# Gate slabs of experts 4 to 15 requested by ScalarE on its own DMA queue

## The chip, the cores and the metric

The kernel runs on one core of a Trainium2 chip. The metric is device time in microseconds (us) of one execution. Work is spread over TensorE (PE), VectorE (DVE), ScalarE (ACT), GpSimd (POOL) and SyncE (SP), and over 16 DMA engines which carry data from HBM into the on-chip memory. SP does no arithmetic here: it waits for semaphores and issues DMA transfers. In the order listings below "ACT" is ScalarE, and a wait `slab_free0` is the semaphore that says that buffer 0 may be overwritten.

## The reference

Two blocks of two layers each, on 256 tokens of width 1024, all in float32. The change touches only the mixture of experts of the first block:

```
def expert_choice_moe(h, w_router, w_gate, w_up, w_down):
    ...
    gates, idx = lax.top_k(aff.transpose(0, 2, 1), cap)      # 16 experts, 32 tokens each
    xs = h[b_ix, idx]
    a = jnp.einsum('becd,edf->becf', xs, w_gate)
    u = jnp.einsum('becd,edf->becf', xs, w_up)
    y = jnp.einsum('becf,efd->becd', jax.nn.silu(a) * u, w_down)
    y = y * gates[..., None].astype(y.dtype)
    return jnp.zeros_like(h).at[b_ix, idx].add(y)
```

Each layer has 16 experts, each with a gate, an up and a down matrix of 1024 x 1024 float32 (4 MB). Before the experts a layer has token mixing, attention over a memory and a router; after the two layers a second block follows, of another kind, with dense matrices.

## The kernel before

**Slabs and slots.** Every matrix of an expert is read as two slabs of 2 MB (2048 KB in the profile), in which each of the 128 partitions gets 16 KB in one piece. The slabs go into a ring of six slots. Gate slabs use slots 0 and 1 (`GATE_SLOTS` is 2), up slabs slots 2 and 3, down slabs slots 4 and 5 (`LAST_SLOT`). So there is one expert's worth of slots, and a slab of the next expert can be asked for as soon as the matmuls that read the slot's old content are done: TensorE then raises `m.free[slot]`, and `ring_wait` waits for it. A transfer raises `m.landed[slot]` by 16 when its last piece is in, and TensorE waits for that (`slab_landed`).

**SP's order.** All slabs are asked for by SP, in one fixed order: `sync_first`, and in it `expert_slabs(e)` for the experts 3 to 14: up, up, down, down of expert e, then gate, gate of expert e+1. Each issue waits for its own slot, so a slot that isn't free holds up all that stand behind it. In layer 0 the loop is written out, and after the experts 3 and 8 two slabs of the next layer's memory weights are asked for (`memory_weights`, 4 KB pieces); in layer 1 it is a loop in registers (`Fori`). Expert 15's up and down slabs follow outside the loop, its second down slab in two halves (`last_down_half`), and then the first slabs of what comes after the experts.

**TensorE's order.** `tensor_experts` runs for expert e: transposes of the gating weights (`turn_places`), then the gate and up products as one nest, k from 0 to 7 outside and the four groups g inside (g 0 and 1 gate, g 2 and 3 up; line 1639). k 0 to 3 need slots 0 and 2, k 4 to 7 need slots 1 and 3. Slots 0 and 2 are free after k = 3, slots 1 and 3 after k = 7. Then it gathers the next expert's tokens, transposes the products, waits for the activation, and runs the down products (line 1673: 16 matmul records for slot 4, 16 for slot 5) and `combine` (line 1683), which adds the expert's rows into the sums of all tokens. In layer 0 the experts 5 to 8 and 11 to 14 are preceded by a piece of other work (`memory_job`, keys and values of the next layer), 7 us on TensorE.

The last expert has an order of its own, `last_gate_up` (line 1568): gate products of k 0 to 3 (slot 0), gate products of k 4 and 5 (slot 1), then, with slot 2, the gate products of k 6 and 7 and the up products of k 0 to 3, then, with slot 3, the up products of k 4 to 7. Its down products for the second slab are done by halves, and `combine` of the first half starts the work that follows the experts.

**ScalarE's order.** `expert` in `scalar_first`: it copies the products out of PSUM (`gu_rows`), applies Silu to the transposed gate products (waits for `gu_T`), and copies the first half of the down product (waits for `dn_full`). TensorE waits for all three. In layer 0 the experts are written out, in layer 1 experts 0 to 14 are a `Fori` loop.

## Time and profile before

| | us |
|---|---|
| median of 3 runs | 2149.88 |
| lowest, highest run | 2148.53, 2151.23 |
| profiled execution, device time | 2150.17 |
| its span (first to last instruction) | 2148.3 |
| TensorE busy in the span | 1886.7 (88%) |
| ScalarE busy | 705.4 (33%) |
| chain that ended last: TensorE | 61% |
| chain that ended last: DMA | 29% |
| of it `w_up` slabs, `w_down` slabs | 17%, 11% |

The chain that ended last is followed back from the end, at each step to what released the waiting instruction. It names what the time went by, so a resource that is busy but not on it costs nothing. The device time is 1.9 us above the span, and the profiled execution lies 0.3 us above the median.

### The profile page before, as it was taken

To read this page: it belongs to the slowest core of one execution; us is meant where nothing else is said; L and a number is where in the kernel's file an instruction comes from. 1 tells how busy PE (TensorE), PEld (TensorE's weight loads), DVE (VectorE), ACT (ScalarE), POOL (GpSimd) and SP (SyncE) were. 2 spreads that over 40 slices of the span, in tenths; PEclk is the share of its full clock that TensorE was granted. 3 is DMA by queue.
4 is the path that set the end of the run, shared out by engine and by line. 5 is a ranking of instruction groups with operands and counts; after the bars stand their busy time and mean duration, and the time that the engine had idled before them with its cause. 6 is when DMAs were issued, how large, how long until landed. Compare 5 with 4: busy or idle time off the path is not lost.

```text
span 2148.3 us, 37589 instructions
## 1 busy us (share of the span) xinstructions
PE 1886.7 (88%) x16744; PEld 1279.0 (60%) x16744; DVE 915.5 (43%) x1340; ACT 705.4 (33%) x1023; POOL 45.7 (2%) x68
## 2 busy tenths in 40 slices
PE   9999958857888999866676689999999999999998
PEld 7897314322325795312222248677999886779997
DVE  7644200101014654101110138458676574486774
ACT  6644100000003653111111135325544454255443
POOL 1000000000000100000000000000000000000000
PEclk9999989989999999988888899999999999999999
DMA  9266999999999358999999995032853360228540
GB/s 340 99 252 254 421 424 427 426 425 428 427 428 390 122 224 345 428 429 428 427 428 429 429 398 185 4 127 94 263 196 138 123 228 4 93 106 276 187 157 20
DMA packets 140159, 592.53 MB, mean 276 GB/s; under 512 B 5840, under 2 KB 59296, under 8 KB 114672
## 3 DMA queue, kind: packets, MB, share of 16 engines
q1 hardware_dynamic: 138912, 586.68, 68.9%
q0 software_dynamic: 1104, 3.70, 0.5%
q8 instruction: 120, 1.97, 0.4%
q14 instruction: 23, 0.19, 0.0%
HBM read 589.30 MB, written 1.05 MB: 275 GB/s over the span
## 4 chain that ended last, share of the span: by engine, by line
PE 61%; DMA 29%; DVE 4%; ACT 2%; SPq 2%; issue 1%; DVEq 0%; POOL 0%; POOLq 0%; ACTq 0%
PE ps L653 37%; DMA ring<-in_w_up 17%; DMA ring<-in_w_down 11%; PE ps L1639 7%; PE ps L3171 3%; PE ps L1673 2%; PE ps L1683 1%; PE ps L3220 1%; SPq L883 1%; PE ps L670 1%; DVE ring_lo L629 1%; DMA area<-in_mem 1%; ACT slab_hi L624 1%; PE ps L3318 1%; PE ps L1212 1%
## 5 line engine op out<-in xcount | busy, mean ns | idle before, releaser
L1639 PE MATMUL ps<-ring,area 128*32 128x512 f32 x1728 | 271.9, 677 | 158.3 <-DMA ring<-in_w_up 157.5
L629 DVE TENSOR_TENSOR ring_lo<-ring,slab_hi 128x2048 fp32r<-128x2048 f32 (+2 forms) x137 | 302.8, 2212 | 182.1 <-ACT slab_hi L624 182.0
L624 ACT ACTIVATE slab_hi<-ring 128x2048 fp32r<-128x2048 f32 (+2 forms) x137 | 253.4, 1852 | 253.1 <-PE ps L653 237.7
L1639 PEld LDWEIGHTS ps<-ring,area 128*32 128x32 f32 x1728 | 64.1, 122 | 324.5 <-DMA ring<-in_w_up 191.0
L653 PE MATMUL ps<-hT_hi,slab_hi 128*128 128x256 f32 x832 | 234.2, 281 | 0.5 <-DVE ring_lo L629 0.5
L653 PE MATMUL ps<-hT_hi,ring_lo 128*128 128x256 f32 x832 | 232.7, 280 | 0.0
L653 PE MATMUL ps<-hT_lo,slab_hi 128*128 128x256 f32 x832 | 232.4, 279 | 0.0
L2021 ACT ACTIVATE area<-ps 128x512 f32<-128x512 f32 x32 | 19.1, 597 | 546.0 <-PE ps L1639 506.3
L2663 DVE COPY area<-ps 128x256 f32<-128x256 f32 x32 | 13.6, 424 | 412.0 <-PE ps L1544 412.0
L1673 PE MATMUL ps<-ring,area 128*32 128x512 f32 x984 | 118.8, 598 | 55.8 <-DVE area L2694 31.0
L653 PEld LDWEIGHTS ps<-hT_hi,slab_hi 128*128 128x128 f32 x832 | 156.5, 188 | 1.3 <-DVE ring_lo L629 1.1
L653 PEld LDWEIGHTS ps<-hT_lo,slab_hi 128*128 128x128 f32 x832 | 156.6, 188 | 0.1
L653 PEld LDWEIGHTS ps<-hT_hi,ring_lo 128*128 128x128 f32 x832 | 156.4, 188 | 0.0
L653 PE MATMUL ps<-ring_lo,hT_hi 128*128 128x512 f32 (+1 forms) x320 | 122.1, 382 | 0.0
L1683 PE MATMUL ps<-area 128*128 128x512 f32 x256 | 118.9, 606 | 1.4 <-ACT area L2025 1.4
L653 PE MATMUL ps<-slab_hi,hT_hi 128*128 128x512 f32 (+1 forms) x304 | 118.2, 389 | 2.1 <-DVE hT_lo L646 0.9
L653 PE MATMUL ps<-slab_hi,hT_lo 128*128 128x512 f32 (+1 forms) x304 | 114.9, 378 | 0.0
L1673 PEld LDWEIGHTS ps<-ring,area 128*32 128x32 f32 x984 | 26.2, 109 | 125.5 <-issue 55.0
L1683 PEld LDWEIGHTS ps<-area 128*128 128x128 f32 x256 | 45.8, 189 | 73.4 <-issue 45.0
L2698 DVE COPY area<-ps 128x512 f32<-128x512 f32 x32 | 22.1, 691 | 143.7 <-PE ps L1673 143.7
L2673 DVE COPY area<-ps 128x256 f32<-128x256 f32 x32 | 13.6, 424 | 153.7 <-PE ps L1561 153.7
L653 PE MATMUL ps<-ring_lo,act_hi 128*128 128x512 f32 x176 | 70.0, 397 | 0.0
(494 smaller groups left out, 3297.9 us busy)
## 6 DMA issues: line engine op xcount, KB each, us to landing
ring<-in_w_down SPq DMA_DIRECT2D x59, 2048.0 KB, 25.9
ring<-in_w_up SPq DMA_DIRECT2D x58, 2048.0 KB, 21.2
ring<-in_w_gate SPq DMA_DIRECT2D x56, 2048.0 KB, 16.0
ring<-in_w_ffn_up SPq DMA_DIRECT2D x44, 1024.0 KB, 8.4
ring<-in_w_in SPq DMA_DIRECT2D x18, 2048.0 KB, 13.4
ring<-in_w_ffn_down SPq DMA_DIRECT2D x10, 2048.0 KB, 7.8
area<-in_w_gate SPq DMA_DIRECT2D x6, 2048.0 KB, 12.7
ring<-in_xattn_w_kv SPq DMA_DIRECT2D x4, 2048.0 KB, 17.2
```

Of the source, the lines that this page charges most:

```text
L624: return m.nc.scalar.activation(hi, whole, ACT.Copy)
L629: return m.nc.vector.tensor_tensor(lo, whole, hi, ALU.subtract)
L653: ins = m.nc.tensor.matmul(out, lhs[a], rhs[b], start=start and i == 0, stop=stop and i == 2, **options)
L670: ins = m.nc.tensor.transpose(m.ps[:, bank + b, k * T + t * P:k * T + (t + 1) * P], src[:, t, cols(k0 + 2 * b + k)], m.ident)
L883: sp.dma_start(slab(m, s, 4, D), expert(name, e, n)).then_inc(m.landed[s], 16)
L1212: ins = mm(ps[:, score_bank(t), h * HD:(h + 1) * HD], m.pT[:, j, kt, :], m.raw[:, kt, c:c + HD], start=kt == 0, stop=kt == 1)
L1639: ins = mm(ps[32 * g:32 * g + CAP, 1, :], m.tokT[:, k, :], rows[:, (g % 2) * BANK:(g % 2 + 1) * BANK], start=k == 0, stop=k == KD - 1)
L1673: ins = mm(ps[32 * c:32 * c + CAP, 2 + nh, :], m.hid[:, c, half, :], rows[:, nh * BANK:(nh + 1) * BANK], start=half == 0, stop=half == 1)
L1683: ins = mm(ps[:, 4 + 2 * nh + t, :], m.pick[:, t * P:(t + 1) * P], m.dn[:, nh, :], start=False, stop=True, skip_group_check=True)
L2698: v.tensor_copy(m.dn[:, 1, :], ps[:, 3, :]).then_inc(s("dn_rows_d"), 1)
L3171: ins = mm(out, m.hT[:, k, tokens], w[:, k, :], start=k == 0, stop=k == KD - 1)
L3220: ins = mm(ps[r, b, u * CH:(u + 1) * CH], lhs[r, u, :], rhs[r, u, :], start=True, stop=True)
```

## The change

In `expert_slabs` SP no longer asks for the gate slabs of expert e+1. ScalarE asks for them, on its own hardware DMA queue: for the experts 3 to 14, right after the Silu of expert e and ahead of the copy that waits for `dn_full`, it waits for slots 0 and 1 and issues the two transfers. The gate slabs of the experts 0 to 3 stay with SP. In layer 1 ScalarE's loop is cut: experts 0 to 2 are written out, 3 to 14 are the loop.

```
--- before.py
+++ after.py
@@ -939,8 +939,6 @@
         into_slots(GATE_SLOTS, up_down, e, e, 3, skipped=1)
         ring_wait(m, sp, LAST_SLOT, HELD_AT[l][LAST_SLOT] + DENSE[l].held[LAST_SLOT] - 1 + e)
         sp.dma_start(slab(m, LAST_SLOT, 4, D), expert("w_down", e, 1)).then_inc(m.landed[LAST_SLOT], 16)
-        into_slots(0, ("w_gate",), e + 1, e - 1)
-
     def memory_weights(j):
...
@@ -2015,12 +2013,17 @@
-    def expert(e):
+    def expert(e, gates=False):
         n = e + (l * E + 1)
         act.wait_ge(s("gu_full"), n)
         go(m.gu, ps[:, 1, :], ACT.Copy).then_inc(s("gu_rows"), 1)
         act.wait_ge(s("gu_T"), n)
         go(m.sil, gate, ACT.Silu).then_inc(s("gate_silu"), 1)
+        if gates:
+            for i in range(GATE_SLOTS):
+                ring_wait(m, act, i, HELD_AT[l][i] + (e - 1) + DENSE[l].held[i])
+                w = m.d["w_gate"].rearrange("l e (h p c) n -> (l e) p h c n", h=2, c=4)[bass.ds(l * E + 1 + e, 1)]
+                act.dma_start(slab(m, i, 4, D), w[:, :, i].rearrange("o p c n -> p (o c) n")).then_inc(m.landed[i], 16)
         act.wait_ge(s("dn_full"), 2 * n - 1)
         go(m.dn[:, 0, :], ps[:, 2, :], ACT.Copy).then_inc(s("dn_rows_a"), 1)
@@ -2039,10 +2042,12 @@
         for e in range(E - 1):
             if e in JOB_AT:
                 memory_job(JOB_AT.index(e))
+            expert(e, gates=e >= 3)
+    else:
+        for e in range(3):
             expert(e)
-    else:
-        with act.Fori(0, E - 1) as e:
-            expert(e)
+        with act.Fori(3, E - 1) as e:
+            expert(e, gates=True)
     expert(E - 1)
```

SP's queue in layer 0, from the down slabs of expert 14 to the first weights after the experts, before:

```order
120 L883 DMA ring<-in_w_down 128x4096 [waits slab_free4]
121 L941 DMA ring<-in_w_down 128x4096 [waits slab_free5]
122 L883 DMA ring<-in_w_gate 128x4096 [waits slab_free0]
123 L883 DMA ring<-in_w_gate 128x4096 [waits slab_free1]
124 L883 DMA ring<-in_w_up 128x4096 [waits slab_free2]
125 L883 DMA ring<-in_w_up 128x4096 [waits slab_free3]
126 L883 DMA ring<-in_w_down 128x4096 [waits slab_free4]
127 L967 DMA ring<-in_w_down 128x4x512 [waits slab_free5]
```

and after:

```order
98 L883 DMA ring<-in_w_down 128x4096 [waits slab_free4]
99 L941 DMA ring<-in_w_down 128x4096 [waits slab_free5]
100 L883 DMA ring<-in_w_up 128x4096 [waits slab_free2]
101 L883 DMA ring<-in_w_up 128x4096 [waits slab_free3]
102 L883 DMA ring<-in_w_down 128x4096 [waits slab_free4]
103 L965 DMA ring<-in_w_down 128x4x512 [waits slab_free5]
```

The two gate slabs of expert 15 are gone from between the down slabs of expert 14 and the up slabs of expert 15.

ScalarE's queue in layer 0 for expert 14 (it begins with the copy that belongs to the memory job), before:

```order
168 L2036 ACTIVATE extra<-ps 128x512 [waits memk_pe]
169 L2021 ACTIVATE area<-ps 128x512 [waits gu_full]
170 L2023 ACTIVATE area<-ps 128x256 [waits gu_T]
171 L2025 ACTIVATE area<-ps 128x512 [waits dn_full]
172 L2021 ACTIVATE area<-ps 128x512 [waits gu_full]
```

and after:

```order
190 L2039 ACTIVATE extra<-ps 128x512 [waits memk_pe]
191 L2019 ACTIVATE area<-ps 128x512 [waits gu_full]
192 L2021 ACTIVATE area<-ps 128x256 [waits gu_T]
193 L2026 DMA ring<-in_w_gate 128x4096 [waits slab_free0]
194 L2026 DMA ring<-in_w_gate 128x4096 [waits slab_free1]
195 L2028 ACTIVATE area<-ps 128x512 [waits dn_full]
196 L2019 ACTIVATE area<-ps 128x512 [waits gu_full]
```

Two transfers now stand between the Silu (`gu_T`) and the copy of the down product (`dn_full`).

ScalarE's queue in layer 1, the loop over the experts, before (a table load stands ahead of either function in every turn):

```order
281 L2021 ACT_TABLE_LOAD
282 L2021 ACTIVATE area<-ps 128x512 [waits gu_full]
283 L2023 ACT_TABLE_LOAD
284 L2023 ACTIVATE area<-ps 128x256 [waits gu_T]
285 L2024 ISA
286 L2025 ACTIVATE area<-ps 128x512 [waits dn_full]
```

and after:

```order
315 L2019 ACTIVATE area<-ps 128x512 [waits gu_full]
316 L2021 ACTIVATE area<-ps 128x256 [waits gu_T]
317 L817 REGISTER_ALU
318 L2026 ISA [waits slab_free0]
319 L2026 DMA ring<-in_w_gate 128x4096
320 L2026 ISA [waits slab_free1]
321 L2026 DMA ring<-in_w_gate 128x4096
```

The loop has the two transfers, and no table load any more: one load now stands ahead of the written-out expert 0.

## Rows read from the trace of the kernel before

**Rows 1.** Stretches of the expert stages: PE, PEld, DVE, ACT, POOL busy; clock, DMA share, GB/s.
```profile
450.00:480.00 30.00, 8.78 (x46) 2.90 (x46) 2.04 (x6) 0.60 (x1) 0.00 (x0) 0.69 1.01 421
630.00:660.00 30.00, 22.89 (x148) 7.09 (x146) 2.44 (x6) 1.58 (x3) 0.00 (x0) 1.00 1.00 425
1150.00:1180.00 30.00, 20.31 (x140) 6.39 (x132) 3.31 (x9) 4.44 (x6) 0.00 (x0) 0.83 1.01 428
```

**Rows 2.** SP's timeline, layer 0: start, time; issues for expert 15.
```profile
627.80 5.22 SPq L883 DMA_DIRECT2D ring<-in_w_gate  x2
633.07 0.91 SPq L883 DMA_DIRECT2D ring<-in_w_up  x2
```

**Rows 3.** PE's timeline, experts 14 and 15 of layer 0; last column idle before, and releaser.
```profile
639.64 1.92 PE L1673 MATMUL ps<-ring,area 128*32 128x512 f32 x16 [1.57 <-DMA ring<-in_w_down]
641.50 3.70 PE L1683 MATMUL ps<-area 128*128 128x512 f32 x8
...
645.35 3.63 PE L1568 MATMUL ps<-ring,area 128*32 128x512 f32 x16
649.43 1.91 PE L1568 MATMUL ps<-ring,area 128*32 128x512 f32 x8 [0.46 <-DMA ring<-in_w_gate]
654.33 3.64 PE L1568 MATMUL ps<-ring,area 128*32 128x512 f32 x24 [2.99 <-DMA ring<-in_w_up]
659.22 1.92 PE L1568 MATMUL ps<-ring,area 128*32 128x512 f32 x16 [1.26 <-DMA ring<-in_w_up]
...
664.73 1.93 PE L1673 MATMUL ps<-ring,area 128*32 128x512 f32 x16 [1.51 <-DVE area L2694]
666.84 1.07 PE L1673 MATMUL ps<-ring,area 128*32 128x512 f32 x8 [0.18 <-DMA ring<-in_w_down]
```

**Rows 4.** ACT's timeline, expert 14 of layer 0: Silu, and the copy after it.
```profile
635.06 0.38 ACT L2023 ACTIVATE area<-ps 128x256 f32<-128x256 f32 x1 [0.94 <-PE ps L1660]
640.77 0.60 ACT L2025 ACTIVATE area<-ps 128x512 f32<-128x512 f32 x1 [5.33 <-PE ps L1673]
```

**Rows 5.** DMA view of 870 to 1240 us: packets; a POOL transfer, KB, us from issue to landing.
```profile
DMA packets 10982, 158.34 MB, mean 428 GB/s; under 512 B 1222, under 2 KB 1222, under 8 KB 1350
area<-in_fix POOLq DMA_DIRECT2D x1, 512.0 KB, 11.7
```

**Rows 6.** DMA view of the whole span: a POOL transfer beside an idle queue, and a small one.
```profile
hT<-in_fix POOLq DMA_DIRECT2D x1, 512.0 KB, 3.9
...
con<-in_consts SPq DMA_DIRECT2D x1, 64.0 KB, 1.9
```

**Rows 7.** POOL's timeline, layer 1: an addition that had waited, a power, and an issue.
```profile
828.38 0.20 POOL L778 TENSOR_TENSOR stat<-stat 128x2 f32<-128x2 f32 x1 [6.27 <-ACT xn L662]
828.65 0.70 POOL L780 TENSOR_TENSOR stat<-stat,con 128x2 f32<-128x2 f32 x1
829.30 0.61 POOL L2214 DMA_DIRECT2D soon<-in_soon  x1
```

**Rows 8.** ACT's timeline, layer 1, expert 14: table load and Silu.
```profile
1232.11 1.28 ACT L2023 ACT_TABLE_LOAD   x1
1233.41 0.38 ACT L2023 ACTIVATE area<-ps 128x256 f32<-128x256 f32 x1
```

**Rows 9.** PE's timeline, layer 1, expert 15: releases by gate and second up slab.
```profile
1247.11 1.91 PE L1568 MATMUL ps<-ring,area 128*32 128x512 f32 x8 [0.47 <-DMA ring<-in_w_gate]
...
1256.90 1.92 PE L1568 MATMUL ps<-ring,area 128*32 128x512 f32 x16 [1.25 <-DMA ring<-in_w_up]
```

**Rows 10.** PE's timeline, layer 0, expert 3: a gap ahead of the products.
```profile
279.90 5.34 PE L1639 MATMUL ps<-ring,area 128*32 128x512 f32 x32 [3.40 <-DMA ring<-in_w_up]
```

**Rows 11.** Short stretches after or around gaps, columns as in rows 1.
```profile
281.00:285.00 4.00, 4.00 (x28) 0.95 (x24) 0.00 (x0) 0.00 (x0) 0.00 (x0) 0.61 1.02 434
652.00:656.00 4.00, 1.67 (x16) 0.53 (x18) 0.00 (x0) 0.00 (x0) 0.00 (x0) 1.00 1.03 438
1220.00:1224.00 4.00, 1.38 (x8) 0.40 (x12) 0.00 (x0) 0.00 (x0) 0.00 (x0) 0.50 0.97 414
```

More of the change, by code:

```diff
@@ L941, in expert_slabs @@
         sp.dma_start(slab(m, LAST_SLOT, 4, D), expert("w_down", e, 1)).then_inc(m.landed[LAST_SLOT], 16)
-        into_slots(0, ("w_gate",), e + 1, e - 1)
     def memory_weights(j):
@@ L2016, in scalar_first, with expert @@
     gate = ps[:, 0, :].rearrange("p (c n) -> p c n", n=P)[:, :, 0:2 * CAP]
-    def expert(e):
+    def expert(e, gates=False):
         n = e + (l * E + 1)
@@ L2023, in expert @@
         go(m.sil, gate, ACT.Silu).then_inc(s("gate_silu"), 1)
+        if gates:
+            for i in range(GATE_SLOTS):
+                ring_wait(m, act, i, HELD_AT[l][i] + (e - 1) + DENSE[l].held[i])
+                w = m.d["w_gate"].rearrange("l e (h p c) n -> (l e) p h c n", h=2, c=4)[bass.ds(l * E + 1 + e, 1)]
+                act.dma_start(slab(m, i, 4, D), w[:, :, i].rearrange("o p c n -> p (o c) n")).then_inc(m.landed[i], 16)
         act.wait_ge(s("dn_full"), 2 * n - 1)
@@ L2041, in scalar_first @@
                 memory_job(JOB_AT.index(e))
+            expert(e, gates=e >= 3)
+    else:
+        for e in range(3):
             expert(e)
-    else:
-        with act.Fori(0, E - 1) as e:
-            expert(e)
+        with act.Fori(3, E - 1) as e:
+            expert(e, gates=True)
     expert(E - 1)
```

## The prediction

> **What bounds the kernel now.** I read the page's slices and its chain of waits first: 29% of the chain is DMA, nearly all of it up and down slabs of the experts. The next view is the busy time by stretches. From 210 to 660 us and again from 850 to 1240 us the DMA share is 1.01 at 428 GB/s in every stretch, even where TensorE does little [rows 1]. So the expert stages are bound by bytes: expert follows expert by what six slabs take. One slab takes 4.89 us (TensorE's successive releases at 649.43, 654.33 and 659.22 [rows 3]), an expert 29.4 us. In such a stage it doesn't matter who asks for a slab, or in which order slabs of one expert come, as long as some transfer is always queued. It matters at one place: at the end, where the last slabs become work that nothing covers. There TensorE's timeline is the view to read, row by row, and beside it the issues of SP and the Silu of ScalarE, which is where the new issues stand.
>
> At that end, before, TensorE is released by the gate slab in slot 1 at 649.43, by the first up slab at 654.33, by the second at 659.22, ends the products at 659.22 + 1.92 = 661.14, starts the down products at 664.73, and ends the first 16 at 666.66; the half slab that it needs next releases it at 666.84 [rows 3]. So the chain of gate and up products has a slack of 0.2 us against the last down slab. Whatever delays these products by more shifts the end of the stage, and what follows is TensorE's own chain (61% of the page's chain), where nothing gives it back.
>
> **The change part by part.**
>
> *Issues taken from SP.* 12 pairs per layer. They cost SP's queue 0.33 to 0.45 us each, with nobody waiting. SP's up slabs are issued right after the gates now (gates 627.80 to 633.02, ups at 633.07 [rows 2]), since slots 2 and 3 come free with slots 0 and 1; without the gates they move up by at most 5 us (the first up slab to 627.8) and queue behind down slabs anyway. Cost 0. What is queued stays enough: at 627.8 slot 3's slab and the two down slabs of expert 14 are still to come, 2 to 3 slabs, 10 us or more.
>
> *Issues added to ScalarE.* They stand behind the Silu, at 635.06 for expert 14, and ahead of the copy of the down product, which starts at 640.77 [rows 4]. Two issues of 0.4 us fit in the 5.3 us for which ScalarE was idle there. Slots 0 and 1 are free by then, so the waits end at once. If an issue were held up until SP's queue had drained (its up issues stood 13 to 15 us at the two places with memory weights), the copy would be late by 10 us, but there TensorE waits 18 us for slabs in any case: in 450 to 480 it is busy for 8.78 us of 30 [rows 1]. Cost 0, bound above 0.5 us.
>
> *Gate slabs are asked for later and travel beside SP's.* Slot 0's slab is asked for at 635.06 instead of 627.80, slot 1's at 635.5 instead of 632.7. And they no longer have the DMA engines for themselves. How two queues share is shown by one transfer of POOL's: 512 KB landed 11.7 us after the issue in the full stage, and 3.9 us beside an idle queue [rows 5, 6]. A transfer is cut into pieces, 8 per engine; in the stage there are (10982 - 1350) = 9632 large ones for 158 MB, 16 KB each [rows 5], so a slab piece holds an engine for 4.89 / 8 = 0.61 us. The 7.8 us extra are 0.98 us for each of POOL's 8 pieces: more than one slab piece, far less than a whole slab (4.89 us) each, and it neither waited for SP's backlog nor went first. I take strict turns, one piece of each queue. Then the 16 pieces of a gate pair are done after 31 or 32 pieces, 19.0 to 19.6 us, and the first 8 after about 9.5 us.
>
> The end of the stage by this: the fixed part of a transfer is 1.9 us for 64 KB [rows 6], less 0.15 us for its bytes, 1.75 us. Slot 1's slab lands at 635.06 + 1.75 + 19.3 = 656.1 instead of 649.4. The second up slab still lands at 659.2, since the bytes ahead of it are the same. For all experts but the last that hides everything: their loop needs slot 1 only together with slot 3. But `last_gate_up` is built on early gates: behind slot 1's slab it still has 1.91 + 3.64 + 1.92 = 7.47 us of products [rows 3] (7.1 if the tails of the records overlap). They end at 656.1 + 7.3 = 663.4 instead of 661.14: 2.3 us late, less the slack of 0.2: **2.1 us per layer**. Bounds: at 654.0 or earlier for slot 1's slab the delay is zero; with 1 us more for start and landing it is 3 us.
>
> *The clock.* The down slab of expert 14 lands up to 2.7 us later too (half rate), so `combine` ends near 648, the gate products of slot 0 run from 648 to 651.8, and TensorE then idles for about 4 us until 656.1. After an idle gap of 3.40 us ahead of 279.90 the granted clock was 0.61 in the next stretch, that is mostly at its lower level of 1.2 GHz, while the gap of 2.99 us ahead of 654.33 left it at 1.00; after the gap of 7.9 us in layer 1 it stands at 0.50 [rows 3, 10, 11]. A gap of 4 us is on the side of the falls, nearest to the 3.40 us one, whose fall lasted about 3.4 us. At half clock that costs the products 1 to 1.7 us, none to 3 us as bounds: **1.2 us per layer**.
>
> *Layer 1.* The same tail: slot 1's release at 1247.11 and the second up slab's at 1256.90 lie 9.8 us apart as in layer 0. The Silu at 1233.41 comes 0.4 us later in it, behind a table load of 1.28 us [rows 8, 9], and without the load it comes as in layer 0. So 2.1 + 1.2 us again. The loads gone from the loop save about 0.4 us per expert on the way to the down products, in a stage that is bound by bytes: 0.
>
> Sum: 2 x (2.1 + 1.2) = 6.6 us. 2150.17 + 6.6 = 2156.8 for the profiled execution, less the 0.3 us by which it lies above the median: **2156.5 us**.
>
> **The rivals.**
>
> *A, late gates, clock stays up.* The mechanism without the fall: 2 x 2.1 = 4.2 us, 2154. For it: `last_gate_up`'s gap of 2.99 us did no harm. Against: 4 us is past the 3.40 us that did.
>
> *B, the gates are in time.* Turns of whole slabs instead of pieces: slot 0's, an up slab, slot 1's, an up slab. From 636.8, with the slab under way done by about 639.5, slot 1's lands three slabs later, at 654.2, and 654.2 + 7.3 = 661.5: 0.2 us of delay within the slack. Or ScalarE's queue hands the transfers out before the Silu is released: slot 1's slab is then issued at 633, first service at 628.7 for slot 0's, and lands near 650. Either gives 2150. Against the first: POOL's 11.7 us; one turn behind at most one slab would have been 3.9 + 4.9 = 8.8 us. Against the second: POOL's issue at 829.30 stands behind two instructions, the first of which had waited 6.27 us, and was not made before they had started, though it needed nothing from them [rows 7]; but that is another engine.
>
> The Trainium skill speaks for the first. Its page "DMA: Bandwidth & Descriptors", section "Queues, rings and completion order", says that an engine drains a whole packet of one ring, typically 9 to 17 descriptors, before it switches; eight pieces would be one turn, and the time that of this rival. POOL's transfer doesn't bear it out, if its pieces were one packet. For the second, the page "Advanced Engine Details and Errata", section "Sequencer Loop", has an engine's instructions wait in a queue while others are read; no run here shows a transfer on ScalarE.
>
> *C, faster.* This is the one on the other side: the table loads that are gone. 12 or 13 turns of layer 1 reach the Silu 0.4 us earlier, and two queues might keep the engines fuller; 13 x 0.4 = 5 us, 2144.6. It decides only where the DMA share of a stretch is below 1, and from 850 to 1240 us there is none [rows 1]. A share of 1.01 leaves two queues nothing to fill.
>
> *D, the flow breaks.* ScalarE's issues are held up behind SP's full queue, or the queues run empty because the down slabs land late and free their slots late. Each of 23 experts would lose a part; with 1 us each 2173. Against: 10 us of queued slabs at the lowest point.
>
> **How the numbers follow.** Forecast 0.38, A 0.15, B 0.31, C 0.07, D 0.09. The likeliest gives 2156.5. The range has to hold forecast, A and B, and the bounds of the two terms: the delay 0 to 3 us and the clock 0 to 3 us per layer would give 2150 to 2162; with 1 us of noise below it is 2149 to 2162, which leaves out C, D and the outermost corner of the forecast. Slower by over 0.2% (above 2154.2; 0.2% is about what a measurement of this kernel can tell from no change): all of the forecast but a little, half of A, D: 0.53. Within it: B, half of A, the rest: 0.40. Faster: 0.07. Forecast and A are alike in sign, so no second range is given.
>
> **What would show it.** Right: gate slabs with a median near 20 us to landing, in a DMA queue of their own; TensorE's row of 8 records (line 1568 before) released by `w_gate` about 3 us before the second up slab, instead of 9.8 us, in both layers; the down products of expert 15 starting 2 to 4 us later after the last up slab; a clock below 1.00 in the stretch around that row; expert after expert still at 29.4 us, DMA share still 1.01. Wrong: slot 1's slab there before 654 in layer 0's time; stretches of the expert stage with a DMA share below 1; ScalarE's copy of the down product later than the down products; table loads still in layer 1's loop.

## The result

The change makes the kernel slower, by far more than the prediction's range allowed.

| | us |
|---|---|
| before, median of 6 runs | 2149.81 (2148.17 to 2151.95) |
| after, median of 6 runs | 2192.81 (2189.44 to 2204.12) |
| ratio, 95% interval | 1.0209 (1.0195 to 1.0222) |
| profiled execution before, after | 2150.17, 2192.74 |
| span before, after | 2148.3, 2190.9 |
| predicted | 2156.5 (2149 to 2162) |

The page of the kernel after, first: the granted clock in 40 slices, the queues, the chain of waits by engine and by line, and the costliest group on TensorE. `q1` is SP's queue, `q10` ScalarE's.

```profile
PEclk9999979888898999988878889999999999999999
...
q1 hardware_dynamic: 132000, 486.01, 57.3%
q10 hardware_dynamic: 6912, 100.67, 10.8%
...
PE 63%; DMA 29%; DVE 4%; ACT 2%; issue 1%; DVEq 0%; SPq 0%; ACTq 0%; POOL 0%; POOLq 0%
PE ps L653 36%; DMA ring<-in_w_gate 25%; PE ps L1637 8%; DMA ring<-in_w_up 3%; PE ps L3176 3%; PE ps L3225 1%; PE ps L1671 1%; PE ps L1542 1%; PE ps L670 1%; PE ps L1681 1%; DVE ring_lo L629 1%; PE ps L1658 1%; DMA ring<-in_w_in 1%; ACT slab_hi L624 1%; PE ps L1566 1%
...
L1637 PE MATMUL ps<-ring,area 128*32 128x512 f32 x1728 | 295.7, 777 | 190.8 <-DMA ring<-in_w_gate 169.0
```

The DMA's share of the chain is 29% as before, but its content is another. Before, it was `w_up` and `w_down` slabs, 17% and 11%; now `w_gate` is 25% and `w_up` 3%. The gate and up products (line 1637 now, 1639 before) wait 169.0 us for gate slabs.

One turn of an expert after, layer 0, first ScalarE, then TensorE (start, time, what ended the idle time before):

```profile
585.96 0.38 ACT L2021 ACTIVATE area<-ps 128x256 f32<-128x256 f32 x1 [0.88 <-PE ps L1658]
585.96 1.64 ACTq L2026 DMA_DIRECT2D ring<-in_w_gate  x2
589.93 0.60 ACT L2028 ACTIVATE area<-ps 128x512 f32<-128x512 f32 x1 [3.58 <-PE ps L1671]
...
617.26 0.38 ACT L2021 ACTIVATE area<-ps 128x256 f32<-128x256 f32 x1 [0.88 <-PE ps L1658]
```

```profile
601.36 3.64 PE L1637 MATMUL ps<-ring,area 128*32 128x512 f32 x32
610.69 5.00 PE L1637 MATMUL ps<-ring,area 128*32 128x512 f32 x32 [5.68 <-DMA ring<-in_w_gate]
615.51 1.04 PE L1542 MATMUL ps<-xn,area 128*32 128x256 f32 x16
...
617.11 0.44 PE L1552 MATMUL ps<-con,area 128*128 128x128 f32 x2
```

This is a closed **ring**. The Silu starts at 585.96, and the pair is issued with it. Slot 1's slab releases TensorE at 610.69, 24.7 us later. The 32 products behind it take 5.00 us instead of 3.64, because the clock fell to half in the gap of 5.68 us ahead of them, and 6.57 us after the release the next Silu starts, which issues the next pair. 24.7 + 6.6 = 31.3 us, against 29.4 us that the bytes of an expert take (with the clock up it would be 24.7 + 3.6 + 1.6 = 29.9 us, an estimate from these rows, 1.6 us being the time from the end of the products to the Silu). The ring is longer, so it sets the pace, and the DMA engines wait for it. Stretches of layer 0 and 1, before and after (us, then busy time of PE, PEld, DVE, ACT, POOL, granted clock, DMA share, GB/s). Before:

```profile
500.00:620.00 120.00, 97.11 (x565) 35.00 (x566) 11.51 (x31) 8.10 (x15) 0.00 (x0) 0.96 1.01 428
950.00:1220.00 270.00, 178.16 (x1154) 56.59 (x1152) 30.45 (x84) 37.30 (x45) 0.00 (x0) 0.85 1.01 429
```

After; the last row is a place in layer 1 where SP's next issue, of the second up slab, waits until 1147.32 for a slot that only the products behind slot 1's gate slab free:

```profile
500.00:620.00 120.00, 90.98 (x534) 31.91 (x538) 11.08 (x32) 7.51 (x14) 0.00 (x0) 0.89 0.98 411
950.00:1220.00 270.00, 179.88 (x1120) 62.17 (x1120) 27.91 (x78) 14.21 (x27) 0.00 (x0) 0.84 0.98 411
...
1146.00:1149.00 3.00, 2.58 (x30) 1.24 (x22) 0.81 (x3) 0.98 (x2) 0.00 (x0) 1.00 0.45 93
```

The stage that ran at a share of 1.01 [rows 1] has dips now: 411 GB/s instead of 428, and 0.45 of the engines in the 3 us from 1146.

**Where the 42.6 us lie** is read from the Silu's starts. Before, those of the experts 8, 9 and 15 of layer 0, then the first and the last of layer 1:

```profile
447.04 0.38 ACT L2023 ACTIVATE area<-ps 128x256 f32<-128x256 f32 x1 [0.94 <-PE ps L1660]
...
488.71 0.38 ACT L2023 ACTIVATE area<-ps 128x256 f32<-128x256 f32 x1 [0.93 <-PE ps L1660]
...
663.25 0.38 ACT L2023 ACTIVATE area<-ps 128x256 f32<-128x256 f32 x1 [1.44 <-PE ps L1656]
...
852.84 0.38 ACT L2023 ACTIVATE area<-ps 128x256 f32<-128x256 f32 x1
...
1260.86 0.38 ACT L2023 ACTIVATE area<-ps 128x256 f32<-128x256 f32 x1 [1.37 <-PE ps L1656]
```

After:

```profile
458.64 0.38 ACT L2021 ACTIVATE area<-ps 128x256 f32<-128x256 f32 x1 [0.88 <-PE ps L1658]
...
490.27 0.38 ACT L2021 ACTIVATE area<-ps 128x256 f32<-128x256 f32 x1 [0.89 <-PE ps L1658]
...
681.27 0.38 ACT L2021 ACTIVATE area<-ps 128x256 f32<-128x256 f32 x1 [1.44 <-PE ps L1654]
...
872.18 0.38 ACT L2021 ACTIVATE area<-ps 128x256 f32<-128x256 f32 x1
...
1304.95 0.38 ACT L2021 ACTIVATE area<-ps 128x256 f32<-128x256 f32 x1 [1.37 <-PE ps L1654]
```

Layer 0: 681.27 - 663.25 = 18.0 us. Between the layers: (872.18 - 681.27) - (852.84 - 663.25) = 1.3 us. Layer 1: (1304.95 - 872.18) - (1260.86 - 852.84) = 24.7 us. Behind it, 1.5 us come back. All of it arises in the two expert stages. Layer 0 loses less because of the memory weights: the Silus of the experts 8 and 9 lie 488.71 - 447.04 = 41.7 us apart before, since two memory slabs travel between, and 490.27 - 458.64 = 31.6 us after. A ring that is longer than the bytes need has room for other bytes. The 11.6 us that layer 0 had lost by expert 8 were down to 1.6 us at expert 9.

### The profile page after: what moved, and what is told of

It reads as the page before. It is cut to its first block, busy times and chain, and to the rows that moved or that the text cites. A ratio compares the mean times of both kernels' runs of the same rounds, so it can differ in the third digit from the quotient of the medians.

```text
span 2190.9 us, 37562 instructions
## 1 busy us (share of the span) xinstructions
PE 1911.8 (87%) x16744; PEld 1289.5 (59%) x16744; DVE 914.0 (42%) x1340; ACT 668.3 (31%) x994; POOL 47.3 (2%) x68
## 3 DMA queue, kind: packets, MB, share of 16 engines
q8 instruction: 120, 1.97, 0.4%
## 4 chain that ended last, share of the span: by engine, by line
PE 63%; DMA 29%; DVE 4%; ACT 2%; issue 1%; DVEq 0%; SPq 0%; ACTq 0%; POOL 0%; POOLq 0%
PE ps L653 36%; DMA ring<-in_w_gate 25%; PE ps L1637 8%; DMA ring<-in_w_up 3%; PE ps L3176 3%; PE ps L3225 1%; PE ps L1671 1%; PE ps L1542 1%; PE ps L670 1%; PE ps L1681 1%; DVE ring_lo L629 1%; PE ps L1658 1%; DMA ring<-in_w_in 1%; ACT slab_hi L624 1%; PE ps L1566 1%
## 5 line engine op out<-in xcount | busy, mean ns | idle before, releaser
L1637 PE MATMUL ps<-ring,area 128*32 128x512 f32 x1728 | 295.7, 777 | 190.8 <-DMA ring<-in_w_gate 169.0
L1637 PEld LDWEIGHTS ps<-ring,area 128*32 128x32 f32 x1728 | 75.0, 137 | 369.4 <-DMA ring<-in_w_gate 175.2
L1671 PE MATMUL ps<-ring,area 128*32 128x512 f32 x984 | 120.0, 622 | 33.9 <-DVE area L2699 28.7
L1671 PEld LDWEIGHTS ps<-ring,area 128*32 128x32 f32 x984 | 29.5, 113 | 100.0 <-issue 69.1
```

The source lines that it names most:

```text
L1637: ins = mm(ps[32 * g:32 * g + CAP, 1, :], m.tokT[:, k, :], rows[:, (g % 2) * BANK:(g % 2 + 1) * BANK], start=k == 0, stop=k == KD - 1)
L1671: ins = mm(ps[32 * c:32 * c + CAP, 2 + nh, :], m.hid[:, c, half, :], rows[:, nh * BANK:(nh + 1) * BANK], start=half == 0, stop=half == 1)
```

## The experiments

The theory that came out of the trace, R: the kernel after is held by the ring of issue, landing, products and Silu; beside it the late pair costs its own share at the last expert of a layer. Rivals: two queues side by side cost something by themselves (S); the lateness of the gate slabs costs the same in one queue (L); the clock's falls are a mere consequence (N); all of the loss lies at the last expert, as the prediction had it.

### The last expert alone

The kernel before, with only expert 15's pair moved: SP leaves it out, and ScalarE asks for it behind expert 14's Silu (the lines of layer 1's loop in ScalarE's program; those of SP's are left out here):

```
...
-        with act.Fori(0, E - 1) as e:
+        with act.Fori(0, E - 2) as e:
             expert(e)
+        expert(E - 2, gates=True)
     expert(E - 1)
```

> Of the 12 pairs per layer only the last one is moved: the gate slabs of expert 15 are asked for by ScalarE behind the Silu of expert 14, all others stay with SP. This is the term that the prediction costed at 2.1 + 1.2 us per layer. Theory R (a ring of waits bounds each middle expert: Silu, issue, two gate slabs at half rate, the products behind slot 1's slab, Silu again): the middle experts are undisturbed, so only the tail is left; with the 24.4 us from issue to release that the changed kernel shows, slot 1's slab comes at 635.1 + 24.4 = 659.5 instead of 649.4 and costs 5.6 us less 0.2 per layer, 2158 to 2164 in all. The prediction's own sizes: 2154 to 2157. Theory E (all 43 us come from the ends of the stages or from ScalarE's queue as such): near 2190.

Measured: 2164.01 us, ratio 1.0054 (1.0038 to 1.0070). TensorE in layer 0:

```profile
649.29 5.32 PE L1570 MATMUL ps<-ring,area 128*32 128x512 f32 x16 [3.26 <-DMA ring<-in_w_gate]
660.05 7.83 PE L1570 MATMUL ps<-ring,area 128*32 128x512 f32 x48 [5.44 <-DMA ring<-in_w_gate]
668.77 1.19 PE L1658 MATMUL ps<-con,area 64*128 64x64 f32 x12 [0.89 <-DVE area L2694]
671.48 1.92 PE L1675 MATMUL ps<-ring,area 128*32 128x512 f32 x16 [1.51 <-DVE area L2702]
```

The pair was issued at 635.07. Slot 1's slab lands at 660.05, 25.0 us later, not at the predicted 656.1, and so behind the second up slab (659.2 before). There is a gap ahead of either gate slab, and in either the clock falls for 3.4 us: 5.32 us for 16 records that took 3.63 [rows 3], 7.83 for 48 that took 6.24 at full clock in the changed kernel, where the second gap was shorter:

```profile
672.92 6.24 PE L1566 MATMUL ps<-ring,area 128*32 128x512 f32 x48 [2.92 <-DMA ring<-in_w_gate]
```

The down products start at 671.48 instead of 664.73 [rows 3], 6.75 us later; twice that is 13.5, and 13.3 us were measured. The mechanism of the prediction's forecast is right in kind, its size was put at half of what it is, and it leaves some 30 us unexplained.

### All but the last expert

The kernel after, with the pair of expert 15 given back to SP at its old place:

```
+        if gates:
+            into_slots(0, ("w_gate",), e + 1, e - 1)
...
-            expert_slabs(e)
+            expert_slabs(e, e == E - 2)
...
-            expert(e, gates=e >= 3)
+            expert(e, gates=3 <= e < E - 2)
...
```

> The changed kernel, but the gate slabs of expert 15, the last one, are asked for by SyncE at their old place; experts 4 to 14 as changed. Theory R: the experts 4 to 14 still come 31 to 32.8 us apart, and only the loss at the end of each layer is gone, 6.7 us per layer as the run with expert 15's pair alone showed: 2192.8 - 13 = 2180 us (2172 to 2186). The prediction's view (all the loss lies at the last expert of a layer): 2150 to 2153 us.

Measured: 2175.82 us, ratio 1.0128 (1.0108 to 1.0149). So 17.0 us of the 43.0 go with the last pair, and 26.0 stay with the other eleven pairs of each layer. The view that all the loss lies at the last expert is out. The two parts, 26.7 us here above the kernel before and 13.3 in the run ahead, make 40.0 of 43.0 us; the interval of the first alone is 4 us to either side.

### The issue earlier, earlier by less, and later

Three kernels move the issue in ScalarE's program and nothing else; the first issues slot 0's slab ahead of the copy of the gate products and slot 1's behind it:

```
+        if gates:
+            gate_slab(0)
         act.wait_ge(s("gu_full"), n)
         go(m.gu, ps[:, 1, :], ACT.Copy).then_inc(s("gu_rows"), 1)
+        if gates:
+            gate_slab(1)
         act.wait_ge(s("gu_T"), n)
         go(m.sil, gate, ACT.Silu).then_inc(s("gate_silu"), 1)
-        if gates:
-            for i in range(GATE_SLOTS):
...
```

> The changed kernel, with ScalarE's issues earlier: slot 0's transfer stands ahead of the copy of the products (it waits for slot 0 alone, free after k = 3), slot 1's right behind that copy, ahead of the Silu. The queue stays ScalarE's, so the slabs still share the DMA engines with SP's. Theory R: the ring gets about 7 us of slack (slot 0's slab starts 7 us earlier), no expert is bound by it and the last expert's gates are in time: 2148 to 2153. Theory S (sharing between two queues is itself the loss, a lower rate or a later start whatever the time of the issue): 2175 to 2195.

The second has the pair behind that copy, and the third behind the copy of the down product (against the changed kernel):

```
         go(m.gu, ps[:, 1, :], ACT.Copy).then_inc(s("gu_rows"), 1)
-        act.wait_ge(s("gu_T"), n)
-        go(m.sil, gate, ACT.Silu).then_inc(s("gate_silu"), 1)
         if gates:
             for i in range(GATE_SLOTS):
...
+        act.wait_ge(s("gu_T"), n)
+        go(m.sil, gate, ACT.Silu).then_inc(s("gate_silu"), 1)
```

```
         go(m.sil, gate, ACT.Silu).then_inc(s("gate_silu"), 1)
+        act.wait_ge(s("dn_full"), 2 * n - 1)
+        go(m.dn[:, 0, :], ps[:, 2, :], ACT.Copy).then_inc(s("dn_rows_a"), 1)
         if gates:
             for i in range(GATE_SLOTS):
...
-        act.wait_ge(s("dn_full"), 2 * n - 1)
-        go(m.dn[:, 0, :], ps[:, 2, :], ACT.Copy).then_inc(s("dn_rows_a"), 1)
```

> The changed kernel with the pair issued right after ScalarE's copy of the gate and up products, ahead of the Silu's wait: 1.5 us earlier than in the changed kernel (584.48 against 585.96 for expert 12), both slabs together as there. If the ring of issue, landing, products and Silu is what holds the experts apart, each of them comes 1 to 1.5 us sooner: 24 turns give 24 to 36 us, so 2157 to 2169 us. If the loss comes from two queues side by side, or from the engines running dry for another reason, 1.5 us of issue change little: 2185 us or more.

> The changed kernel with the pair issued behind ScalarE's copy of the down product: 4.0 us later than in the changed kernel (589.93 against 585.96 for expert 12). By the ring every one of the 24 turns grows by up to 4.0 us; SyncE's queue is emptier by then, so that the pair may land a little sooner after its issue: 70 to 96 us more, 2260 to 2290 us. If the experts were held by anything else, less than 20 us more, below 2213 us.

The kernel with the issue 4.0 us later was run twice, the two others seven and four times.

| issue, against the Silu's start | us | ratio |
|---|---|---|
| slot 0's 5.0 to 7.1, slot 1's 1.5 us earlier | 2156.20 | 1.0031 (1.0018 to 1.0045) |
| both 1.5 us earlier | 2167.95 | 1.0087 (1.0070 to 1.0104) |
| with it (the change) | 2192.81 | 1.0209 (1.0195 to 1.0222) |
| both 4.0 us later | 2257.61 | 1.0502 (1.0481 to 1.0523) |

The time follows the moment of the issue: 24.9 us for 1.5 us in 24 turns (1.0 us per turn), 64.8 us for 4.0 us (2.7 per turn; 70 us or more had been expected). In the last kernel the stage falls to 371 GB/s:

```profile
500.00:620.00 120.00, 89.53 (x512) 31.01 (x505) 11.51 (x31) 7.50 (x14) 0.00 (x0) 0.86 0.91 371
```

With slot 0's slab ahead of the copy the ring has slack, and the bytes set the pace again: in layer 1 the Silus of the experts 4 to 14 are 29.4 us apart on every turn, and in layer 0, where the turns are uneven, expert 14's is at 634.83 (635.06 before). What is left, 5.5 us in all (the total is 3 us above the expected range), is at the ends of the layers. The second down slab of expert 14 shares the engines with the early gate pair and lands late, so the last expert's products begin at 653.38 and run through without a wait:

```profile
646.03 3.57 PE L1671 MATMUL ps<-ring,area 128*32 128x512 f32 x16 [7.77 <-DMA ring<-in_w_down]
649.53 3.70 PE L1681 MATMUL ps<-area 128*128 128x512 f32 x8
653.07 0.38 PE L1559 MATMUL ps<-con,area 128*128 128x128 f32 x2
653.38 9.67 PE L1566 MATMUL ps<-ring,area 128*32 128x512 f32 x64
```

They end at 663.05 instead of 661.14 [rows 3]. The same tail costs 3.8 us in layer 1.

### Early issue, and the last pair with SP

Both remedies in one kernel, `gate_slab(0)` and `gate_slab(1)` around the copy for the experts 4 to 14, and SP's `into_slots` for expert 15, with the lines shown for each above:

> The changed kernel with both remedies: for the experts 4 to 14 ScalarE issues slot 0's slab ahead of its copy of the gate products and slot 1's right behind that copy (some 5 us before the Silu), and expert 15's gate slabs are SyncE's at their old place. If the loss of the changed kernel consists of the ring (issue to landing to Silu) and of the late pair at the last expert, and of nothing else, both are gone: 2148 to 2152 us. If two queues cost something of their own per expert, or the earlier issue alone left a loss that isn't at the last expert: 2155 us or more.

Measured: 2151.70 us, ratio 1.0007 (0.9995 to 1.0019). The two parts account for the whole loss; beyond some 4 us, the upper end of the interval, nothing is left for two queues by themselves. It doesn't beat the kernel before either: the bytes bind both.

### One slab of the pair

The kernel after, with slot 0's slab asked for by SP at its old place, and only slot 1's by ScalarE behind the Silu:

```
+        ring_wait(m, sp, 0, HELD_AT[l][0] + (e - 1) + DENSE[l].held[0])
+        sp.dma_start(slab(m, 0, 4, D), expert("w_gate", e + 1, 0)).then_inc(m.landed[0], 16)
...
-            for i in range(GATE_SLOTS):
+            for i in (1,):
                 ring_wait(m, act, i, HELD_AT[l][i] + (e - 1) + DENSE[l].held[i])
...
```

> The changed kernel with half of the change: slot 1's gate slab is asked for by ScalarE after the Silu, as in the changed kernel, slot 0's by SyncE at its old place. Only one slab then takes turns with SyncE's, so it should land some 13 to 14 us after the Silu, as slot 0's did in the changed kernel, instead of 24.4. Theory R (ring bound by the 24.4 us): the ring is 14 + 5 + 1.7 = 21 us and no longer binds; the bytes do, at 29.4 us per expert, and at the end of each layer slot 1's slab is in time as well: 2148 to 2158 us. Rival S (two queues side by side cost time by themselves, each expert 1 us or more, however little is asked for in the second): 2170 us or more.

Measured: 2148.99 us, ratio 1.0004 (0.9991 to 1.0017): no difference, with the issue as late as in the changed kernel. The view of the DMA issues (KB each, median us from issue to landing), and the stretches:

```profile
ring<-in_w_gate SPq DMA_DIRECT2D x32, 2048.0 KB, 19.8
ring<-in_w_gate ACTq DMA_DIRECT2D x24, 2048.0 KB, 13.9
```

```profile
630.00:660.00 30.00, 23.00 (x146) 7.78 (x140) 2.44 (x6) 1.58 (x3) 0.00 (x0) 0.94 1.00 426
1150.00:1180.00 30.00, 20.29 (x132) 6.29 (x128) 3.21 (x9) 1.58 (x3) 0.00 (x0) 0.83 1.01 428
```

Slot 1's slab takes 13.9 us to landing when it is alone in the second queue, and some 24.5 us behind slot 0's. At 13.9 + 6.6 = 20.5 us the ring is far below the 29.4 us of the bytes, and at the last expert of layer 0 both gate slabs have released TensorE by 649.07, as early as before (649.43 for slot 1's). Rival S is out: the second queue is in use in every one of the 24 turns here and costs nothing. The half change is free and the whole costs 43 us, because beside SP's queue a transfer in the second one proceeds at about half rate, and only two slabs one behind the other make the ring too long.

### The clock's part

Three kernels give TensorE idle work in its gaps: small matmuls whose results are not used (a and b stand for the counts, and the definition of `fill` is left out).

```
+        if middle and l:
+            fill(a)
         for k in range(0 if last else KD):
+            if middle and k == 4:
+                fill(b)
```

The first had a = 16 and b = 12.

> The changed kernel, with extra matmuls that nobody reads in TensorE's two gaps of the middle experts: 12 of 128 x 256 between k = 3 and k = 4 in both layers, and 16 ahead of the nest in layer 1 (0.22 us each at full clock). Theory R: the products behind slot 1's slab (5.3 to 6.4 us in the changed kernel, 3.6 at full clock) lie in the ring, so a clock that stays up takes 1.7 to 2.7 us out of each expert until the bytes bind at 29.4: 2155 to 2175. Theory N (the clock is a symptom, the ring is no bound): 2190 or more.

Measured: 2192.00 us, ratio 1.0192 (1.0177 to 1.0206), at a clock of 1.00 in the stretches of layer 1. The total is in rival N's range, but it decides nothing: in layer 1 TensorE itself had become the bound, with 28.47 us busy of 30 from 1058 to 1088. Each filler is two matmul records, so they took 7.15 and 5.45 us per expert:

```profile
1067.61 7.15 PE L1631 MATMUL ps<-con 128*128 128x256 f32 x32 [0.61 <-DVE area L2688]
1074.69 3.64 PE L1647 MATMUL ps<-ring,area 128*32 128x512 f32 x32
1078.26 5.45 PE L1631 MATMUL ps<-con 128*128 128x256 f32 x24
1083.64 3.64 PE L1647 MATMUL ps<-ring,area 128*32 128x512 f32 x32
```

The second had a = 7 and b = 6.

> The changed kernel, with idle matmul work on TensorE that keeps it busy in its two gaps per expert: 6 small matmuls (some 2.7 us) ahead of k = 4 in experts 3 to 14, and in layer 1 another 7 (some 3.1 us) ahead of the nest. Their result is not used. The fill of the run before this one was so long that TensorE itself became the bound. Theory R (a self-timed ring: Silu, issue on ScalarE, 24.4 us to the landing of slot 1's slab, its products at half clock because of the gap before them, Silu): with the products at full clock, 3.64 us instead of 5.3 to 6.5, the ring is 24.4 + 3.64 + 1.7 = 29.7 us, near the 29.4 us of the bytes, so the experts come 29.4 to 30.2 us apart and the kernel takes 2155 to 2172 us. Rival N (the clock is a consequence only; the late slabs and dry queues hold the experts apart at 31 to 32.8 us whatever TensorE does in its gaps): 2185 us or more.

Measured: 2185.57 us, ratio 1.0179 (1.0155 to 1.0202). The total is in rival N's range again, and the clock still fell ahead of most of the products. But it did so in some turns and not in others, in one kernel. Here are the products behind slot 1's slab for the experts 12 and 13 of layer 0:

```profile
578.38 5.14 PE L1647 MATMUL ps<-ring,area 128*32 128x512 f32 x32 [3.25 <-DMA ring<-in_w_gate]
610.19 3.64 PE L1647 MATMUL ps<-ring,area 128*32 128x512 f32 x32 [3.26 <-DMA ring<-in_w_gate]
```

Either pair of slabs took 25.1 us from the Silu to the release. The first turn, at half clock, is 31.8 us from Silu to Silu, the second, at full clock, 30.3. From the Silu of expert 4 to that of expert 14 of layer 0, apart from the turn with memory weights, the three turns with products of 3.64 us take 29.8 to 30.3 us and the six with slower ones 31.5 to 33.2. In layer 1 the two with products of 3.64 us take 29.6 and 29.7 us, the other nine 30.7 to 32.6. (The next expectation says that every gap of this length was followed by half clock; the one ahead of 610.19 was not.)

The third had a = 7 and b = 9.

> The changed kernel with 9 small matmuls of unused work (some 4.1 us) ahead of k = 4 in experts 3 to 14, and in layer 1 another 7 (some 3.1 us) ahead of the nest. In the run with 6 and 7 the gap ahead of k = 4 was still 3.25 to 3.29 us and each was followed by 3.4 us of half clock, so it decided nothing; with 9 the gap should be some 1.9 us and the clock stay up. Theory R, with the clock as a term of the ring: landing 24.4 us after the Silu, products at full clock 3.64 us, 1.7 us to the Silu: 29.8 to 30.7 us per expert instead of 31.2 to 32.9, so 2158 to 2175 us. Rival N (what holds the experts apart is only the landing, which comes later by as much as TensorE gets faster): 2182 us or more.

Measured: 2182.30 us, ratio 1.0144 (1.0121 to 1.0166). The total is where rival N had it. The trace says why that total is no verdict. In layer 0 the clock stays up:

```profile
554.00:584.00 30.00, 27.47 (x164) 12.17 (x162) 3.19 (x9) 2.18 (x4) 0.00 (x0) 1.00 1.00 420
1050.00:1080.00 30.00, 24.93 (x156) 12.17 (x157) 2.48 (x9) 1.20 (x2) 0.00 (x0) 0.94 0.98 416
```

```profile
579.03 3.64 PE L1647 MATMUL ps<-ring,area 128*32 128x512 f32 x32 [1.69 <-DMA ring<-in_w_gate]
```

There the Silus of the experts 9 to 13 come 30.9, 30.1, 30.0 and 30.2 us apart, instead of 31.5, 32.8, 31.4 and 31.3: the ring is 24.8 + 5.3 = 30.1 us. Layer 1 has both kinds side by side: of the 11 turns from expert 3 to 14, the three in which the clock stayed up took 29.4, 29.4 and 29.8 us, and the eight in which it fell once, for 3.4 us, 30.5 to 31.4. Against that stand costs of the fill itself: 3.8 and 3.6 us at expert 3 of each layer, where nothing was idle, and some 8 us at the memory weights of layer 0, whose bytes (39.6 us from Silu to Silu, 31.6 after) no longer fit into a ring with less slack. So single turns show the clock's part, and there rival N is out: the turns get shorter by 1 to 3 us where the clock stays up, and the landing doesn't move. In the changed kernel the products behind slot 1's slab take some 2 us above 3.64 on the mean, and its turns (without those of the memory weights) exceed 29.4 us by 2.7 us in layer 0 and 2.1 in layer 1. By an estimate from its rows (each turn at full clock would be its time to the release plus 3.64 and 1.6 us, or 29.4 where that is more) the half clock makes up 40 of the 47 us that these 20 turns exceed 29.4 by. So the late landing uses up the slack, and most of what is lost on top is the clock. The clock's part of the 43 us as a whole is not measured: the totals of all three filled kernels missed theory R's range.

The kernel with the issue 1.5 us earlier is mixed: its runs were 2158.69, 2166.63, 2169.27 and 2169.57, and in the profiled one, the fastest, the clock still falls in nearly every turn (0.83 of full clock from 950 to 1220, as in the changed kernel's 0.84). Four turns of layer 0 have no gap ahead of k = 4. Of the five that have one of 3.0 to 3.7 us there, one kept its clock, and it took 27.7 us, where the two before it took 30.6 and 30.5:

```profile
571.30 3.64 PE L1637 MATMUL ps<-ring,area 128*32 128x512 f32 x32 [3.19 <-DMA ring<-in_w_gate]
```

### Late, but in one queue

The kernel before, SP alone, but its gate slabs issued only once the Silu has ended:

```
+        sp.wait_ge(m.s("gate_silu"), e + (l * E + 1))
         into_slots(0, ("w_gate",), e + 1, e - 1)
```

> The kernel before, with the gates still asked for by SP, but only once the Silu of the same expert has ended (one wait on its semaphore ahead of them). So the issue is as late as in the changed kernel, and there is one queue. Theory R: lateness alone costs nothing, since the two slabs travel at full rate behind at most the rest of the down slabs: 2148 to 2153. Theory L (an issue at the Silu is too late whoever makes it): 2185 to 2195.

Measured: 2164.04 us, ratio 1.0062 (1.0047 to 1.0078), between the two expectations, so each was wrong here. Most of the cost of the change isn't lateness as such (L is out), but lateness isn't free: a wait in SP's queue also holds up the up slabs behind the gates, though it is not shown that this is what costs the 13 us. Layer 0, two stretches behind one late issue (at 580.53):

```profile
580.00:584.00 4.00, 2.29 (x19) 0.62 (x18) 0.75 (x2) 0.38 (x1) 0.00 (x0) 1.00 1.00 406
584.00:588.00 4.00, 1.82 (x16) 0.42 (x16) 0.00 (x0) 0.60 (x1) 0.00 (x0) 1.00 0.97 381
```

By the transfer records some engines run out of pieces there while others still have some, and 40 of the 297 pieces that start from 580 to 592 take 0.65 to 2.3 us instead of 0.615. The turns lose 0 to 2 us, irregularly. Why the pieces are long is open.

### The loop's cut alone

The kernel before, with only ScalarE's loop of layer 1 cut as in the change:

```
-        with act.Fori(0, E - 1) as e:
+        for e in range(3):
+            expert(e)
+        with act.Fori(3, E - 1) as e:
             expert(e)
```

> The kernel before, with only ScalarE's loop of layer 1 cut as in the change (experts 0 to 2 written out, 3 to 14 the loop), all gate slabs with SyncE. The table loads of 1.28 us inside the loop should be gone. If the stage is bound by bytes everywhere, nothing is gained: 2149 to 2151.5 us, the experts of layer 1 still 29.4 us apart on the mean. The prediction's rival C (the loads cost 0.4 us in each of 12 or 13 turns): 2144.6 to 2146 us.

Measured: 2150.24 us, ratio 1.0004 (0.9995 to 1.0013). Two rows of expert 13 show that the table load between copy and Silu is gone (the Silu follows after 0.93 us of waiting for TensorE), and nothing is gained by it. The rule for rival C, that the loads lie in a stage bound by bytes, held.

```profile
1203.27 0.60 ACT L2021 ACTIVATE area<-ps 128x512 f32<-128x512 f32 x1 [22.91 <-PE ps L1639]
1204.80 0.38 ACT L2023 ACTIVATE area<-ps 128x256 f32<-128x256 f32 x1 [0.93 <-PE ps L1660]
```

## Why the prediction was wrong

**What bounds the kernel now: right.** The stage before is bound by bytes, and giving the gates another queue changes nothing as long as some transfer is always queued; the runs with one slab, and with the early issue, confirm it. (Its "428 GB/s in every stretch" was 421 to 429, and 410 in the first.)

**"For all experts but the last that hides everything": the step that failed.** The prediction found that the loop needs slot 1 only together with slot 3, compared the landing with the up slabs of the same turn, and stopped there. But the change had tied the issue to the Silu, and the Silu comes after the products, which come after the landing. Such a dependence has to be summed once around. With the prediction's own landing time and the products at full clock that gives 21.0 + 3.6 + 1.6 = 26.2 us (1.6 from the end of the products to the Silu), which is below 29.4. So the sum would have let it pass, with only 3 us of slack, and two of its terms were undersized:

- *Landing.* 23.8 to 25.0 us were needed in the middle experts, where 21.0 were predicted. The turns were right: 32 pieces by 0.61 are 19.5 us, and by the transfer records the pair's pieces take 19 to 20.4 us from the first start to the last end in the middle experts. Wrong was the fixed part of 1.75 us, from a small transfer beside an idle queue [rows 6]. In the busy stage the first piece starts 3.4 to 3.8 us after the issue in all 24 pairs, and in most of them the landing is seen 1.0 to 1.1 us after the last piece.
- *Products.* 3.64 us at full clock became 4.9 to 6.6 us (6.9 once), as the clock fell around the gap of 3.2 to 5.9 us ahead of them each time. The prediction applied this to the last expert only. With the landing alone corrected the ring is 29.0 to 30.2 us, about what the bytes take; it is this term that makes it 31 to 33.

Layer 0: 24.7 + 4.9 to 6.6 + 1.6 = 31.2 to 32.9 us, against 31.2 to 32.95 in the trace. Layer 1: 24.3 + 5.0 to 6.9 + 1.6 = 30.9 to 32.8, against 30.7 to 32.8.

**The last expert: right in kind, 13.3 us instead of 6.6.** The same two terms are at fault. With that pair alone moved, slot 1's slab lands 4 us later than predicted, behind the second up slab, and slot 0's is late too (649.29 against the predicted start of its products at 648), so there are two gaps, with two falls of the clock, where the prediction had one.

**"Issues taken from SP. Cost 0": wrong in one point.** "10 us of queued slabs at the lowest point" was read off the kernel before. After, SP's up issues wait for slots that products behind a gate slab free, so SP's queue runs empty with them (93 GB/s from 1146 to 1149). It is a consequence of the ring, not a cost of its own: it goes with the early issue.

**"Issues added to ScalarE. Cost 0": right.** In layer 0's turn shown above, the copy of the down product starts 3.97 us after the Silu, right behind TensorE's products.

**The rivals.** D, at a chance of 0.09, was nearest: its mechanism (slots freed late, each of 23 experts losing a part) is what happened, though from another cause, and its price of 1 us per expert was a guess. The measured turns lose 1.3 to 3.6 us. The argument against it, the queued slabs, presumed the flow of before. B is out in both forms. Turns of whole slabs: in the 5 us from 465 the transfer records have SP's queue on 0.47 of the engines and ScalarE's on 0.53, and from 470 on 0.52 and 0.50, slot 0's slab is 13.8 to 15.2 us on its way, slot 1's about 24 from the same Silu. The 5 us alone could hide whole turns of some engines against others; in stretches of 0.61 us from 464.4 to 469.3, one piece's time, ScalarE's queue has 0.33, 0.73, 0.28, 0.72, 0.28, 0.72, 0.28, 0.72 of the engines, which is piece by piece. By the typical packet that the Trainium skill names ("DMA: Bandwidth & Descriptors", "Queues, rings and completion order"), 9 to 17 descriptors, slot 1's would have come after some 19 us, as in the prediction's working; the measurement decides, for pieces of 16 KB. Issue ahead of the Silu: the issue has the Silu's start as its own (585.96, 585.96), so it goes out when the Silu's wait ends and didn't overtake it. C is out by the loop's cut.

**The range** was made of the two terms' bounds at one place, and the sum of a term that occurs 23 times had been set to zero with no bound at all. One microsecond of doubt there is worth 23; a range that held this would have had to reach 2193.

## What to carry to other kernels

When a transfer's issue moves behind an instruction, follow the data from the issue to the landing, through the work behind it and back to that instruction, sum it once around, and compare with what paces the loop now; a slack of a tenth is none. Take the latency from a transfer made in the same traffic, and the work's time at the clock that the new gap leaves. Two transfers of 2 MB in a row in a second queue arrived at half rate beside a full first one, the second of them 24 us after the issue instead of 14: moving only one of them was free here, and asking for the first 5 to 7 us and the second 1.5 us earlier took away what the ring cost in the middle experts.

## What was new of the hardware

- The first piece of the pair asked for in ScalarE's queue started 3.4 to 3.8 us after its issue in all 24 turns of the changed kernel; SP's own, issued into an idle queue in the same execution, 0.99 and 0.95 us (issues at 1147.32 and 1242.71). It is not a property of ScalarE's queue: in the kernel with the early issue four of the 24 started after 0.99, 1.04, 2.10 and 2.69 us, the first two where SP's next slab was issued just behind ScalarE's (358.96 and 359.01, 547.37 and 547.43) and SP's queue had less than a slab left. That the 3.5 us are a wait behind what SP's queue had already handed out fits this, and is not shown.
- Two queues shared the engines evenly, piece by piece (16 KB, 0.61 us), for as long as both had work.
- The length of a single gap doesn't decide whether the clock falls. With a = 7 and b = 6 it fell around the gap of 3.25 us ahead of 578.38 and stayed up over that of 3.26 ahead of 610.19. With a = 7 and b = 9 layer 1 has ten gaps of 1.97 to 1.99 us ahead of k = 4, each with another of 1.5 to 2.3 us some 10 us before it; the clock fell at seven of them and stayed up at three. Two turns of it, with a fall in the first:

```profile
1063.83 3.73 PE L1647 MATMUL ps<-ring,area 128*32 128x512 f32 x32 [2.01 <-DMA ring<-in_w_gate]
1073.63 5.34 PE L1647 MATMUL ps<-ring,area 128*32 128x512 f32 x32 [1.99 <-DMA ring<-in_w_gate]
...
1105.15 3.64 PE L1647 MATMUL ps<-ring,area 128*32 128x512 f32 x32 [1.98 <-DMA ring<-in_w_gate]
```
